# Order of the row gathers in the expert stage: four rows of u, then the four rows of v of the same experts

## The reference, cut to what matters

```
eidx = jnp.take_along_axis(cand_idx, pos, axis=-1)      # 16 experts per token and head
g = jax.nn.softmax(top_s, axis=-1)
u = expert_u[eidx]
h = jnp.einsum('btd,bthkd->bthk', xblk, u)
act = jax.nn.gelu(h, approximate=False) * g
return jnp.einsum('bthk,bthkd->btd', act, expert_v[eidx])
```

## Time and profile before

| | us |
|---|---|
| median of 3 runs | 3719.93 |
| lowest and highest | 3708.38, 3737.2 |
| profiled execution | 3748.34 |
| its span | 3746.5 |

### The profile page before, as it was taken

How to read it: one execution, slowest core, us unless ns; L and a number is a source line. 1 busy time by engine, 2 the same in 40 slices (tenths; PEclk the granted TensorE clock), 3 DMA queues, 4 the chain that set the end, 5 groups by cost and what they waited for, 6 DMA issues and landing times. The chain is left out here.

```text
span 3746.5 us, 50783 instructions
## 1 busy us (share of the span) xinstructions
PE 3234.4 (86%) x18906; PEld 2588.8 (69%) x18906; DVE 2395.2 (64%) x4712; ACT 1457.6 (39%) x2874; POOL 1238.6 (33%) x1211
## 2 busy tenths in 40 slices
PE   6997788777789968887877799999999999999999
PEld 6894344443268944444432599888999998898899
DVE  6776666655557555655666565877666656767565
ACT  3642222222236412222221344565554444565543
POOL 1306677777623056776777200010000000000000
PEclk7998899988899988888988899999999999999999
DMA  7669999999976489999999654434355554334354
GB/s 294 212 222 349 380 366 384 382 365 358 331 280 207 141 335 360 368 373 361 377 357 361 228 183 152 147 119 141 130 170 185 183 183 141 130 135 135 131 185 163
DMA packets 258290, 937.14 MB, mean 250 GB/s; under 512 B 29312, under 2 KB 30720, under 8 KB 257792
## 3 DMA queue, kind: packets, MB, share of 16 engines
q0 software_dynamic: 161280, 587.27, 41.6%
q1 hardware_dynamic: 96768, 346.62, 27.1%
HBM read 932.73 MB, written 1.05 MB: 249 GB/s over the span
## 5 line engine op out<-in xcount | busy, mean ns | idle before, releaser
L695 PE MATMUL M<-rows,diag 128*128 128x512 f32 x2048 | 984.7, 638 | 350.9 <-ACT diag L919 257.8
L695 PEld LDWEIGHTS M<-rows,diag 128*128 128x128 f32 x2048 | 413.4, 205 | 882.1 <-issue 873.1
L268 DVE TENSOR_TENSOR w_low<-ring,w_high 128x1024 fp32r<-128x1024 f32 x560 | 685.9, 1228 | 415.0 <-ACT w_high L260 412.4
L1210 DVE CUSTOM_DVE_ANT_0 rows<-rows,attn 128x1024 f32<-128x1024 f32 x512 | 615.6, 1223 | 463.6 <-DMA rows<-in_expert_u_dram,expert 414.3
L287 PE MATMUL G<-x_high,w_high 128*128 128x256 f32 x2576 | 764.5, 297 | 50.0 <-DVE w_low L268 17.0
L290 PE MATMUL G<-x_high,w_low 128*128 128x256 f32 x2576 | 741.4, 288 | 0.0
L260 ACT ACTIVATE w_high<-ring 128x1024 fp32r<-128x1024 f32 x560 | 588.6, 1054 | 349.0 <-PE G L287 324.2
L289 PE MATMUL G<-x_low,w_high 128*128 128x256 f32 x2448 | 706.1, 288 | 0.0
L412 POOL DMA_INDIRECT rows<-in_expert_v_dram,expert x512 | 557.0, 1088 | 279.4 <-issue 129.6
L412 POOL DMA_INDIRECT rows<-in_expert_u_dram,expert x512 | 548.1, 1070 | 302.1 <-issue 154.5
L287 PEld LDWEIGHTS G<-x_high,w_high 128*128 128x128 f32 x2576 | 507.6, 197 | 63.6 <-issue 38.4
(11 more groups left out here) (360 smaller groups left out, 4779.8 us busy)
## 6 DMA issues: line engine op xcount, KB each, us to landing
ring<-in_stream_dram SPq DMA_DIRECT2D x654, 512.0 KB
ada_ring<-in_ada_stream_dram POOLq DMA_DIRECT2D x80, 512.0 KB, 4.9
rows<-in_ada_stream_dram POOLq DMA_DIRECT2D x16, 512.0 KB
rows<-in_expert_u_dram,expert POOLq DMA_INDIRECT x512
rows<-in_expert_v_dram,expert POOLq DMA_INDIRECT x512
const<-in_const_dram SPq DMA_DIRECT2D x1, 1096.5 KB, 11.2
x<-in_x_dram SPq DMA_DIRECT2D x1, 1024.0 KB, 5.4
out_dram<-x SPq DMA_DIRECT2D x8, 128.0 KB, 3.5
```

Of the source, the lines that this page charges most:

```text
L268: dve.tensor_tensor(T["w_low"][:, part, :], T["ring"][:, place.slot(chunk, slots), :], T["w_high"][:, part, :].bitcast(F32), ALU.subtract) ...
L695: mm = pe.matmul(M[:, 2 * t + half, :], T["diag"][:, n % 4, :], T["v_rows"][:, n % SLOTS, half * 512:(half + 1) * 512], start=(h == 0 and ...
L1210: dve.tensor_tensor_reduce(row, row, T["x_tok"][:, t, :], 1.0, 0.0, ALU.mult, ALU.add, T["hid"][:, r, k:k + 1]).then_inc(sem["u_used"], 1)
```

## The change

The loop over single steps becomes a loop over groups of four. For each group GpSimd issues the four gathers of u, then the four gathers of v of the same steps. The order is now u0 to u3, v0 to v3, u4 to u7, v4 to v7, and so on. The number of gathers, the waits in `gather`, the buffers and all other engines' programs stay.

```diff
-            experts, behind = ROUNDS * TOPK, SUB
-            for n in range(experts + behind):
-                if n < experts:
-                    r, k = divmod(n, TOPK)
-                    if k == 0:
-                        pool.wait_ge(sem["routed"], r + 1)
+            for at in range(0, ROUNDS * TOPK, SUB):
+                r, first = divmod(at, TOPK)
+                if first == 0:
+                    pool.wait_ge(sem["routed"], r + 1)
+                for k in range(first, first + SUB):
                     gather(T["expert_u"], T["u_rows"], rows["u_landed"], sem["u_used"], r, k)
-                if n >= behind:
-                    r, k = divmod(n - behind, TOPK)
+                for k in range(first, first + SUB):
                     gather(T["expert_v"], T["v_rows"], rows["v_landed"], sem["v_used"], r, k)
```

## The result

| | kernel before | changed kernel |
|---|---|---|
| median, us (four runs each, one chip) | 3718.37 | 3806.43 |
| lowest and highest | 3708.38, 3737.2 | 3792.11, 3809.45 |
| profiled execution, span | 3748.34, 3746.5 | 3804.89, 3803.1 |

The ratio is 1.0239, with a 95% interval of 1.02 to 1.0279: 88 us slower, where +96 was forecast. What follows accounts for the 56.6.

The account below looks back on a forecast made before the run. The expert stages were taken to wait for rows, with slots of v nearly too few across a route. Thirty rounds growing 3.2 us each gave +96 us, other terms zero: 3719.93 + 96 = 3816 us, range 3735 to 3870.

Parts of the forecast that it names:

- The slots of v run short: Expert stages: slots of v are already nearly too few across a route, with 3.3 us spare a round.
- the spare: Round with a route: 3.3 us from the end of the group's matmuls to the gather of v(11), paying part of the delay.
- 3.2 us a round: Growth of each round with a route: 6.2 + 0.3 - 3.3 us, in 30 rounds +96 us.
- The third piece: From the gather of v(11) to the end of u(19)'s product: 18.3 us before, to grow by 6.2 us.
- The 26.3 us: From product(3) to the end of its group's matmuls, across the route: forecast to stay at 26.3 us.
- From v(11) to u(19), five more gathers: GpSimd's queue behind the wait for v(3)'s slot: 12 gathers instead of 7, costing 5 x 1.24 = 6.2 us.
- The other groups: zero: Slack of v falls 6.2 us everywhere, but groups beyond the one ending in v(11) were forecast to add zero.
- v(15): Last gather of v in a round: 7.8 us in hand, or covered by its round's own stall; cost zero.
- Rival 3: Every group stalls because TensorE is late outside routes too: a further 96 us, 3912 us; chance 0.08.
- VectorE and GpSimd together: zero: Gathers meeting VectorE's products, now four in a row: bounds -143 and +46 us, taken as 0.
- rival 2: Not slower: gathers run at 0.94 us in VectorE's pauses, giving 3744 or 3673 us; chance 0.12, 0.07 for faster.
- Rival 1, the pace of the transfers: Bandwidth sets the expert stages' 1.51 us a gather, so order means nothing: no change, 3720 us; chance 0.18.

Follow-up runs that it names:

- the fourth experiment: Groups of four as in the changed kernel, but with v's gathers one group later, against the kernel before on chip A: 3594.0 us, ratio 0.9896.

## Why the prediction came out right, step by step

**The slots of v run short: right.** Ten slots bring the time back to that of before (0.9997), and the waits fell by as much as the time. The table is read from the timelines, over the rounds from the second to the last but one. Hold is the mean time from the gather of a row of v to the end of its matmuls, spare the mean from there to the next gather into that slot; "late" is the share of gathers issued within 0.35 us of their release. The distance is the number of gathers from u(n) to v(n) in the queue, by the order written in the loop.

| kernel | distance | hold, us | spare, us | late |
|---|---|---|---|---|
| before (chip of the result) | 9 | 17.7 | 6.1 | 4% |
| changed (same chip) | 4 | 22.4 | 2.8 | 24% |
| changed (A) | 4 | 22.1 | 2.4 | 32% |
| turns, two behind (A) | 5 | 21.5 | 3.5 | 11% |
| groups, v one group behind (A) | 12 | 16.5 | 5.1 | 8% |
| turns, six behind (C) | 13 | 13.9 | 9.5 | 0% |

A row of v is used when the product of its step, the weights and the diagonal are done. Asked for earlier it isn't used earlier, it only holds its slot longer. Hold and spare together are the time of eight steps (21.6 to 25.2 us), and so the spare is what is left for stalls such as the route or the query projections. The mean alone doesn't order the two kernels at distance 4 and 5 on chip A: there the count from v(8) to u(19) does, 15 against 17.

**"3.2 us a round": the pieces as forecast, the sum a little too large.** The third piece grew by 5.7 us (6.2 forecast), the spare went from 3.3 to 0.37 us (to 0.3 forecast), and a round came to 50.3 us, 2.4 more and not 3.2. Over the 28 rounds that is 67 us; the windows show 52.7, so by subtraction what lies outside these rounds came out some 14 us shorter. The 26.3 us stayed, at 26.0. The waits of GpSimd on TensorE rose by 138 us, where about 100 was forecast; all its waits on semaphores rose by 104. The layer's 512 gathers took 803.5 and 795.2 us, less than the 820 forecast, at 349 and 354 GB/s, forecast 343.

That +96 came so close to +88 is in part luck. The prediction had one term that was not zero. The traces have five: waits on TensorE +138.4, shorter gathers -44.4, fewer of the stops called "remote" -27.8, gaps called issue -7.2, waits on VectorE -6.2, together +52.8. The other 31 us of the 88 lie between the profiled executions and the medians, and no trace explains them. On chip A the same change cost 129.

**"From v(11) to u(19), five more gathers": the wrong gather.** In this group v(8) stops first and longest: in the changed kernel the waits on TensorE at v(8) are 42.5 and 39.8 us in the two layers, those at v(10) 23.5 and 28.1, those at v(11) 9.2 and 10.4. As the gathers stand one behind the other, v(11) is at the end of a stall that others began. The count by v(11) gave +60 for the turns with v two behind, and +160 was measured. The count by v(8) puts the kernels in the right order, but it prices them too low: v(8) had 1.5 us of spare before (mean of the 28 rounds), so that two gathers more cost 2 x 1.24 + 0.3 - 1.5 = 1.3 us, +39 in 30 rounds, and four more +113, where 129 and 160 were measured on that chip. So 3.2 us a round was close to what was measured, but its five gathers are not what the stall consists of.

**"The other groups: zero": wrong, but not where it looked.** Waits of the gathers of v on TensorE, both layers, by the place of the waiting gather in its round (us, read from the timelines):

| kernel | v(0) to v(3) | v(4) to v(7) | v(8) to v(11) | v(12) to v(15) |
|---|---|---|---|---|
| before | 10.0 | 7.4 | 69.3 | 11.8 |
| changed | 5.0 | 46.9 | 182.6 | 2.3 |
| changed, on A | 4.3 | 37.3 | 184.8 | 1.2 |
| before, no route (B) | 5.5 | 23.3 | 16.0 | 14.1 |
| changed, no route (B) | 4.0 | 23.4 | 62.9 | 34.1 |
| changed, route later (B) | 1.2 | 18.1 | 63.2 | 122.4 |

Of v(15) the prediction was right: behind the stall of its own round it waits for almost nothing. What it left out is v(4) to v(7), which take the slots of the last four steps of the round before: 39.5 us more than before, over a quarter of the rise. Without any route the changed order still costs 85 us, about two thirds of the 129 on a chip of that kind, and then v(8) to v(11) and v(12) to v(15) wait longer than in the order before. With the route two steps later the waits come up at v(12) to v(15) and the time stays. TensorE's own work between steps, the 3.62 us of projections, is enough for such a stall. Rival 3 had this mechanism, but expected it on top of +96. It came in its place, since a stall in one group gives the next one time. How much of the loss each group would have by itself is not settled by these runs.

**"VectorE and GpSimd together: zero": wrong in size.** The gathers became 44.4 us shorter in sum, about a third of rival 2's upper bound of 143 us. It was not, as rival 2 had it, that many gathers moved into the pauses: 429 started inside a product before and 397 after. Those last 1.246 us on average before and 1.166 after, any other 0.95 to 0.96. The prediction's reading of the earlier trace rows was right and holds throughout: sorted by the point of the product at which they start, the gathers end 0.81 us (median) behind the product's end, before and after alike, for starts in its first 1.2 us. So an early start costs up to 1.99 us, one in the product's last 0.2 us about 0.97. In the first 0.8 us of a product 170 gathers started before, 110 after.

**Rival 1, the pace of the transfers: wrong for this kernel.** The stage ran at 365 GB/s before, slower still (349) when the order changed, and at 405 in the fourth experiment, on chip A. The Trainium skill has two figures for this path. By "SBUF — State Buffer", section "A bandwidth-pool intuition that's wrong (but worth ruling out)", about 358 GB/s per core is given for the path from HBM; as a ceiling for this one busy core, the trace disagrees with 405 over 694 us. By "DMA: Bandwidth & Descriptors", section "Measured (HBM→SBUF, 128 partitions, SWDGE, issued from GpSimd)", one core whose neighbour is idle reached 425 GB/s; the trace's 409 lies near it. Only where nothing else stops the gathers does this ceiling show.

**The difference between chips** stays partly open. The change costs 3.5% on A and 2.4% on the chip of the result. On the latter the gathers were also stopped by "remote", 51.3 us before and 23.5 us after, so some of what the slots now cost lies where the kernel had stopped anyway; that is an argument and no run shows it. Whether the 1.0 to 1.2% of the fourth experiment come from the grouping or from asking for v later isn't told apart either: the turns with v six behind ran on C only, and the groups with eight slots on A and B only.

## What to carry to other kernels

Where two streams share one in-order queue and one of them is used later, ask for the later one as late as its landing allows: a slot costs its holding time, and holding time, not the number of waits, is to be compared with slots times the pace. A buffer whose waits are short (98.5 us of 1546 here) may have only a few microseconds in hand; count, for each waiting gather of a group and not only for the last, how many gathers lie between it and the one that the consumer needs next. When a fix moves a wait without shortening the stage, as the later route did, the shortage is of slots and not of the place where it shows.

## What the runs showed of the hardware

- One core gathers rows of 4 KB at 405 to 408 GB/s for a whole stage (694 and 689 us; 409 in single slices), with a median of 11.7 us from issue to landing once the requests queue up, against 6.6 us where the slots hold them back.
- The same kernel takes 3631 and 3637 us on two chips and 3713 and 3718 us in the other two sets of runs, 2.1 to 2.4% more. In the slower ones GpSimd stops 14 to 37 times (23.5 to 76.7 us in sum, up to 4.6 us each) at gathers whose slot is free, which the profile calls "remote"; no trace of the faster ones shows such a row at the gathers. The kernel before was not profiled on those, and their traces hold landing times where those of the slower ones don't, so the two kinds of trace are not alike in all.
- A gather that GpSimd starts inside a product of VectorE (1.22 us) ends 0.81 us behind the product's end, wherever in the product's first 1.2 us it started; undisturbed it lasts 0.94 us.
